# A delta-rule unit's schedule moved by two slots, and some of its VectorE work given to ScalarE

## The reference, cut to what matters

```python
L = jnp.where(strict, jnp.einsum('bhncd,bhnjd->bhncj', k_beta, k) * decay, 0.0)
a = L + jnp.eye(C, dtype=jnp.float32)
sol = lax.linalg.triangular_solve(a, rhs, left_side=True, lower=True)
u, w = sol[..., :DV], sol[..., DV:]
...
v_new = u_n - jnp.einsum('bhcd,bhde->bhce', w_n, state)
o = jnp.einsum('bhcd,bhde->bhce', q_n, state) + jnp.einsum('bhcj,bhje->bhce', attn_n, v_new)
state = state * jnp.exp(gl)[..., None, None] + jnp.einsum('bhcd,bhce->bhde', k_n, v_new)
```

## Time and profile before

| | |
|---|---|
| time of the kernel, median of 3 runs | 2789.07 us (2785.65 to 2792.15) |
| time of the profiled execution | 2786.32 us |
| its span | 2784.5 us |
| TensorE busy | 2702.4 us (97%) |
| TensorE weight load busy | 2256.1 us (81%) |
| VectorE busy | 1725.8 us (62%) |
| ScalarE busy | 561.3 us (20%) |
| GpSimd busy | 885.8 us (32%) |
| mean granted TensorE clock | 0.992 of full speed |

### The profile page before, as it was taken

The page is one execution under the profiler, slowest core; times in us unless marked ns, Lnnn a source line. Parts: engine busy times, 40 slices in busy tenths (PEclk is TensorE's granted clock), DMA queues, the critical chain, the costliest instruction groups (busy, mean ns, idle before and its releaser), DMA issues.

```text
span 2784.5 us, 38178 instructions
## 1 busy us (share of the span) xinstructions
PE 2702.4 (97%) x14098; PEld 2256.1 (81%) x14098; DVE 1725.8 (62%) x3816; ACT 561.3 (20%) x1207; POOL 885.8 (32%) x471
## 2 busy tenths in 40 slices
PE   7899999999999999999998999999999999999998
PEld 5788888888888888788777888888888888887886
DVE  5788788878854333433567797878877434443333
ACT  5222222222211111200141222222222111121001
POOL 3333233323312212434442232323333122133443
PEclk9999999999999999999999999999999999999999
DMA  4322222222211112333422322222222111133344
GB/s 164 90 64 69 67 80 64 67 66 81 70 48 39 36 40 63 125 95 114 155 82 77 81 58 74 70 77 69 62 73 75 42 46 33 40 100 96 98 132 144
DMA packets 288476, 217.71 MB, mean 78 GB/s; under 512 B 31426, under 2 KB 245780, under 8 KB 288036
## 3 DMA queue, kind: packets, MB, share of 16 engines
q1 hardware_dynamic: 255330, 154.39, 20.3%
q10 hardware_dynamic: 32962, 60.89, 6.4%
HBM read 176.37 MB, written 38.86 MB: 77 GB/s over the span
## 4 chain that ended last, share of the span: by engine, by line
PE 61%; DVE 18%; DMA 8%; issue 5%; POOL 4%; SPq 3%; ACT 1%; DVEq 0%; ACTq 0%; POOLq 0%
PE dense_ps L688 16%; PE dense_ps L692 16%; PE dense_ps L690 16%; DMA arena<-l_scratch 6%; SPq L578 2%; PE work L671 2%; DVE arena L1535 2%; DVE arena L1775 2%; DVE arena L1778 1%; DMA l_scratch<-arena 1%; DVE arena L1549 1%; POOL w_lo L2007 1%; PE work L874 1%; PE work L854 1%; POOL arena L2091 1%
## 5 line engine op out<-in xcount | busy, mean ns | idle before, releaser
L688 PE MATMUL dense_ps<-act_hi,w_hi 128*128 128x512 f32 x2816 | 1174.2, 417 | 15.9 <-POOL act_lo L2124 9.2
L692 PE MATMUL dense_ps<-act_hi,w_lo 128*128 128x512 f32 x2816 | 1106.3, 393 | 0.0
L690 PE MATMUL dense_ps<-act_lo,w_hi 128*128 128x512 f32 x2816 | 1105.0, 392 | 0.0
L2007 POOL TENSOR_TENSOR w_lo<-w_raw,w_hi 128x1024 fp32r<-128x1024 f32 x192 | 495.2, 2579 | 1328.2 <-DVE w_hi L1412 1328.2
L692 PEld LDWEIGHTS dense_ps<-act_hi,w_lo 128*128 128x128 f32 x2816 | 531.6, 189 | 117.7
L688 PEld LDWEIGHTS dense_ps<-act_hi,w_hi 128*128 128x128 f32 x2816 | 534.2, 190 | 111.6 <-POOL act_lo L2124 11.8
L690 PEld LDWEIGHTS dense_ps<-act_lo,w_hi 128*128 128x128 f32 x2816 | 534.6, 190 | 89.6 <-issue 0.2
L1535 DVE SCALAR_TENSOR_TENSOR arena<-arena,cols 128x512 f32<-128x512 f32 x288 | 273.9, 951 | 4.9
L1412 DVE CAST w_hi<-w_raw 128x1024 fp32r<-128x1024 f32 x192 | 132.9, 692 | 208.8 <-PE dense_ps L692 194.7
L671 PE MATMUL work<-mk,arena 128*128 128x128 f32 x896 | 130.3, 277 | 11.5 <-issue 7.5
L1775 DVE TENSOR_TENSOR arena<-arena 128x60 f32<-128x60 f32 (+14 forms) x480 | 99.8, 208 | 53.9 <-DMA arena<-l_scratch 41.7
(11 more groups left out here) (194 smaller groups left out, 3208.2 us busy)
## 6 DMA issues: line engine op xcount, KB each, us to landing
w_raw<-in_w_in SPq DMA_DIRECT2D x142, 512.0 KB, 3.7
arena<-l_scratch SPq DMA_DIRECT2D x32, 512.0 KB
gate_scratch<-arena ACTq DMA_DIRECT2D x64, 256.0 KB, 2.5
arena<-gate_scratch ACTq DMA_DIRECT2D x64, 256.0 KB, 2.9
w_raw<-in_w_out SPq DMA_DIRECT2D x18, 512.0 KB, 4.2
arena<-row_scratch SPq DMA_DIRECT2D x32, 256.0 KB, 5.3
o_scratch<-arena ACTq DMA_DIRECT2D x32, 256.0 KB, 2.0
arena<-o_scratch ACTq DMA_DIRECT2D x32, 256.0 KB, 3.3
```

What stands on the lines that cost most here:

```text
L688: eng.matmul(dense_ps[:, to, :], w_hi[:, slot, k, :], hi[:, k, seg], start=(k == 0), stop=False)
L690: eng.matmul(dense_ps[:, to, :], w_hi[:, slot, k, :], lo[:, k, seg], start=False, stop=False)
L692: mm = eng.matmul(dense_ps[:, to, :], w_lo[:, slot, k, :], hi[:, k, seg], start=False, stop=(k == KT - 1))
L2007: eng.tensor_tensor(w_lo[:, slot, :, :], w_from[second][:, :, :], w_hi[:, slot, :, :].bitcast(F32), ALU.subtract)\
```

## The change

1. **Slots.** In `even`, `odd` and `even_last` the solve goes from slots 3 to 7 to slots 5 to 9, `spread` from 8 to 10, the level steps from 9 to 17 to 11 to 19; in `first` the solve goes from 17 to 21 to 19 to 23 and the rest with it. `mask` and `dec` of the following unit go from 12 and 14 to 10 and 12 in `even` and `odd`; in `first` from 15 and 17 to 18 and 20, and `gram`, `keys`, `nl` of the second unit from 21, 23, 24 to 25, 26, 27. The slots without convolution steps are those of the solve, as before.
2. **ScalarE.** The copies of `level_v` 1 and 2 and of `level_x` 1 and 2, and within the units the rounding of the weight blocks (`split_hi`), are done by ScalarE.
3. **SP.** In the first unit the stores of the L blocks stand ahead of the load of weight block 3 and of the second row load; `lb` is loaded behind that weight block, and the row last.
4. `spread` has one more wait (for `xT` of the unit before, now written by ScalarE), and the first rounding of the first retention head waits for ScalarE's last one.

```diff
@@ unit_schedule, first
-        at(15, "mask", 1)
         at(16, "kq")
-        at(17, "dec", 1)
-        at(21, "gram", 1)
-        at(23, "keys", 1)
-        at(24, "nl", 1)
-        solve, spread_at, vt = 17, 22, 34
+        at(18, "mask", 1)
+        at(20, "dec", 1)
+        solve, spread_at, vt = 19, 24, 34
@@ the other kinds
-        solve, spread_at, vt = 3, 8, 19
+        solve, spread_at, vt = 5, 10, 19
+    else:
+        solve, spread_at = 0, 0
...
+    if first:
+        begin(25, 1)
...
     if kind in ("even", "odd"):
-        at(12, "mask", 1)
-        at(14, "dec", 1)
+        at(10, "mask", 1)
+        at(12, "dec", 1)
         begin(16, 1)
...
-            spread(0 if 3 <= n < 8 else 1 if n < 18 and n not in (12, 15) else 2)
+            spread(0 if solve <= n < spread_at else 1 if n < 18 and n not in (12, 15) else 2)
@@ sync
                 row_load(0, 0)
+                l_store(0, 0)
+                load_w(n + BLK_FIRST + 3, w_src(l, w_in, GR0))
+                l_load(0)
                 row_load(0, 1)
-                load_w(n + BLK_FIRST + 3, w_src(l, w_in, GR0))
-                l_blocks(0, 0)
@@ scalar
+                def split_hi(g, slot):
+                    eng.wait_ge(w_in_ok.sem, w_in_ok.after(g, 16))
+                    eng.wait_ge(dense_ok[1].sem, dense_ok[1].after(g, -1))
+                    eng.wait_ge(w_hi_ok.sem, w_hi_ok.after(g, 0))
+                    eng.activation(w_hi[:, slot, :, :], w_raw[:, :, :], ACT.Copy).then_inc(w_hi_ok.sem, 1)
...
+                        elif what == "split":
+                            idx = g0 + step[1] + 1
+                            split_hi(g + idx, idx % 2)
+                        elif what == "level_v" and step[1]:
+                            i = step[1]
+                            eng.wait_ge(v_ps.sem, v_ps.after(tn, i + 1))
+                            eng.wait_ge(xp_ps.sem, xp_ps.after(tn, i))
+                            w = 3 * P // 4 if i == 1 else LVW
+                            eng.activation(vv[0:w], wk[4][0:w, 0:CPH * LVW].rearrange("p (c t) -> p c t", c=CPH), ACT.Copy)\
+                               .then_inc(vv_ok.sem, 1)
+                        elif what == "level_x" and step[1]:
+                            ...
+                            if i == 1:
+                                eng.activation(xT[nb][0:32, :, 32:64], new[0:32, :, 0:32], ACT.Copy)
+                                eng.activation(xT[nb][64:96, :, 96:128], new[32:64, :, 32:64], ACT.Copy).then_inc(xt_ok.sem, 1)
+                            else:
+                                eng.activation(xT[nb][0:LVW, :, LVW:P], new[0:LVW], ACT.Copy).then_inc(xt_ok.sem, 1)
@@ vector
-                        elif what == "split":
-                            idx = g0 + step[1] + 1
-                            split_w(g + idx, idx % 2)
...
                         elif what == "spread":
                             eng.wait_ge(sv_s.sem, sv_s.after(tn, 2 * BASE - 2))
+                            eng.wait_ge(xt_ok.sem, xt_ok.after(tn, 0))
...
                 def ret_head(h, last):
                     m = (n + h * 6)
+                    if h == 0:
+                        eng.wait_ge(w_hi_ok.sem, w_hi_ok.after(m + BLK_RET + 5, 0))
                     split_w(m + BLK_RET + 5, (BLK_RET + 5) % 2)
```

More of the change, by code:

```diff
@@ L569, in row_load, with l_store @@
                        .then_inc(row_in.sem, 16)
-                def l_blocks(u, half):
+                def l_store(u, half):
                     t = (l * (2 * DH) + u)
@@ L578, in l_blocks, with l_load @@
                         eng.dma_start(l_dram[a].rearrange("c i k -> i c k"), nl[half][seg, :, seg]).then_inc(l_st.sem, 16)
+                def l_load(u):
+                    t = (l * (2 * DH) + u)
                     eng.wait_ge(l_st.sem, l_st.after(t, 16 * NB))
@@ L582, in l_blocks @@
                                   .to_broadcast([NB, BASE, CPH * BASE * BASE])).then_inc(l_in.sem, 16)
+                def l_blocks(u, half):
+                    l_store(u, half)
+                    l_load(u)
                 row_load(0, 0)
+                l_store(0, 0)
+                load_w(n + BLK_FIRST + 3, w_src(l, w_in, GR0))
+                l_load(0)
                 row_load(0, 1)
-                load_w(n + BLK_FIRST + 3, w_src(l, w_in, GR0))
-                l_blocks(0, 0)
                 load_w(n + BLK_HEADS, w_src(l, w_in, DK0 + P))
@@ L1227, in delta_unit @@
                                 ret_v(l * RH, gg, int(of[2]), half)
+                        elif what == "split":
[9 more added lines that the diff above has]
+                        elif what == "level_x" and step[1]:
+                            i = step[1]
+                            new = wk[5][:, 0:CPH * LVW].rearrange("p (c t) -> p c t", c=CPH)
+                            eng.wait_ge(xp_ps.sem, xp_ps.after(tn, i + 1))
+                            if i == 1:
[3 more added lines that the diff above has]
+                                eng.activation(xT[nb][0:LVW, :, LVW:P], new[0:LVW], ACT.Copy).then_inc(xt_ok.sem, 1)
                         elif what == "tanh":
@@ L1741, in delta_unit @@
                             i = step[1]
-                            eng.wait_ge(v_ps.sem, v_ps.after(tn, i + 1))
                             if i == 0:
+                                eng.wait_ge(v_ps.sem, v_ps.after(tn, i + 1))
                                 level = mk[:, C_LV + i * LVW:C_LV + (i + 1) * LVW].unsqueeze(1).to_broadcast([P, CPH, LVW])
@@ L1746, in delta_unit @@
                                                   ALU.mult).then_inc(vv_ok.sem, 1)
-                            else:
-                                eng.wait_ge(xp_ps.sem, xp_ps.after(tn, i))
-                                w = P - LEVELS[i]
-                                eng.tensor_copy(vv[0:w], wk[4][0:w, 0:CPH * LVW].rearrange("p (c t) -> p c t", c=CPH))\
-                                   .then_inc(vv_ok.sem, 1)
                         elif what == "level_x":
                             i = step[1]
-                            eng.wait_ge(xp_ps.sem, xp_ps.after(tn, i + 1))
-                            new = wk[5][:, 0:CPH * LVW].rearrange("p (c t) -> p c t", c=CPH)
                             if i == 0:
+                                eng.wait_ge(xp_ps.sem, xp_ps.after(tn, i + 1))
                                 part = lower(xT[nb].rearrange("p c t -> p (c t)"), i)
@@ L1759, in delta_unit @@
                                                   ALU.add).then_inc(xt_ok.sem, 1)
-                            elif i == 1:
-                                eng.tensor_copy(xT[nb][0:32, :, 32:64], new[0:32, :, 0:32])
-                                eng.tensor_copy(xT[nb][64:96, :, 96:128], new[32:64, :, 32:64]).then_inc(xt_ok.sem, 1)
-                            else:
-                                eng.tensor_copy(xT[nb][0:LVW, :, LVW:P], new[0:LVW]).then_inc(xt_ok.sem, 1)
                         elif what == "solve":
```

## The result

The changed kernel takes 2869.7 us in the median (2868.8 to 2870.2) against 2789.2 us before (2785.7 to 2792.2): ratio 1.0288, 95% interval 1.0268 to 1.0308, so it is 2.9% slower. One run of the changed kernel was disturbed (4498.8 us, clock 0.56) and is left out. The profiled execution took 2868.8 us with a span of 2867.0 us, 82.5 us more than the one before.

The account below looks back on a forecast made before the run. TensorE, busy for 2702 of 2784 us, was taken to bound the kernel. Old waits -24, solve held by GpSimd +117, clock +24 and first units -5 gave +112 on the median 2789.1: 2901 us, range 2765 to 2955.

Parts of the forecast that it names:

- the likeliest case: Whole kernel: the forecast that GpSimd holds the solve, 2901 us, own range 2850 to 2950, chance 0.55.
- The solve meets GpSimd: From slot 8: `w_lo`, starting at 17.0 us, and both masks hold solve steps on VectorE; +117 us (93 to 138).
- What it costs, 3.9 us a unit: TensorE's waits for `uu` and `spread`: 3.9 us a unit (3.1 to 4.6), 30 units, +117 us.
- -24 us for the old waits: Solve two slots later: the wait on `lb` and TensorE's before L904 and L915 go, -24 us (-30 to 0).
- +24 us for the clock: TensorE's clock falls behind the new waits: 0.8 us each, 30 times, +24 us.
- Rounding at slot 0: On ScalarE, ahead of the copy of the new values: costs TensorE 0 to 0.2 us a unit, taken as 0.
- rival C: ScalarE as new obstacle: copy behind rounding, tanh behind `dec`, up to 1 us a unit; 2790 us, chance 0.05.
- First units, -5 us: First unit of each layer: shorter waits and clock loss, -10.5, less 5.5 for masks holding the solve; -5 (-15 to +5).
- Masks two slots earlier, 0: Masks and `dec` two slots earlier: moves nothing by itself, 0, bounds -0.3 and +0.5 us a unit.
- What counts is what the rounding released.: Second rounding on ScalarE at slot 8 no longer follows solve and `spread`, so `w_lo` and masks meet the solve; +117 us.
- Rival A: No meeting: solve over before GpSimd matters, or short instructions slip in between; only gains stay, 2763 us, chance 0.22.

Follow-up runs that it names:

- rounding back on VectorE: Changed kernel with the unit roundings back on VectorE in its order; slots, level copies and SyncE's order as changed: 2936.1 us.
- slots of before: Changed kernel with the earlier kernel's slots (solve from slot 3, `spread` at 8); roundings and level copies still on ScalarE, SyncE's order as changed: 2756.6 us.
- second rounding behind `spread`: Changed kernel with the second rounding kept on ScalarE but moved from slot 8 to 11, waiting for `spread`; mask and `dec` at 12 and 14: 2870.7 us.
- one more GpSimd instruction: Changed kernel with one more GpSimd instruction of 128x512 behind the masks (the second mask written twice): 2924.5 us.
- first unit unheld: Against slots of before: in first units, masks in slot 22 waiting for `spread`, later `dec`, `gram`, `keys`, `nl`; weight block HEADS+1 loaded ahead of the stores: 2749.5 us.

## Why the prediction was right, and where its numbers were off

The class and the mechanism were right: forecast 2901 us, measured 2869.7, inside the range and inside the likeliest case's own (2850 to 2950). That the number came as near as 31 us is in part luck: units and clock were put 44 us too high (141 against 97.3 us, the holds of the first even units included), and 15.7 us came from a wait that the sum does not have.

- **The solve meets GpSimd.** Right, to the instruction: `w_lo` was put 17.0 us behind the unit's start, and it came at 17.5 (475.44 - 457.91). The three holds of 2.2, 0.9 and 1.0 us above the normal length are there in the unit shown, and three such in every even and odd unit. Taking the masks away, adding one instruction, and moving the solve by one slot changed the number of holds as counted.
- **What it costs, 3.9 us a unit.** The mis-sized term. The 28 ordinary units lose 90.0 us, 3.2 each, restarts of TensorE and clock included, where I had 4.7 with the clock. The step that failed is the count "at +2.1 nine small instructions are left" and that `uu` "stands behind the third of them": seven were left, and `uu` stood behind the first, so it was out at +2.7 us from the start of `w_lo` and TensorE waited 1.0 us for it, not 4.5. The other two holds cost 1.2 us at `level_v` 0, since GpSimd was through 4.9 us from the start of `w_lo`, not 5.4. I had 3.9 us for a VectorE that is two instructions ahead, which it was; there I had left `uu` behind the second hold by mistake, when two ahead puts it behind the first.
- **-24 us for the old waits.** Right: the loss of all 30 units before was 27.8 us, and its causes are gone (L914 1.0 us, no wait on `lb`).
- **+24 us for the clock.** Wrong, near 0 in ordinary units: waits of 1.0 and 1.2 us left it at 1.00. It follows at least in part from the size above: with waits of 1.0 and 2.2 us it fell to 0.50 in 10 of 18 units, and behind one of 3.1 us or more in all 28 even and odd units of the run with the rounding back on VectorE. The mean clock of the profile is 0.990 (0.992 before).
- **Rounding at slot 0, "0 to 0.2 us a unit".** Right in the ordinary units, wrong in the two first even ones, where the block had not landed. I had ruled that SP's other queue entries keep their order; they do, but one of them stood behind stores that wait for the moved `nl`. That is +15.7 us, rival C in one place. I had moved a step without following the queue it feeds.
- **First units, -5 us.** -3.3 us. The masks fell on the convolution ahead of the solve (three L1571 took 6.15 us together), and the `w_lo` of the next block (92.90 us) on the solve, 2.27 us on k=11; TensorE's wait is 5.34 us against 5.62.
- **Masks two slots earlier, 0.** Right, by the run that puts them back.
- **"What counts is what the rounding released."** Half right. Released early, `w_lo` is the better place for it as long as the solve is over by then: that alone made the kernel before 18.8 us faster (2766.9 against the 2785.7 us measured beside it). It hurts only together with the solve's two slots, and the slots hurt more without it (2936 us). Rival A's own condition, a `w_lo` later against the solve, is met with the solve two slots earlier, and A's number (2763) is near what came (2757), though not by A's sum: A has 5 to 10 us from the first units, which gave 0.7 us there.

The Trainium skill, page "SBUF — State Buffer" (section "SBUF: two separate sides"), says that whichever of the two starts first holds the pair for its whole instruction and the other fully blocks. Every hold shown here agrees, the one of four elements a partition (L1844, 1.24 us) too, which a sharing of bandwidth could not stretch so. One thing does not, as far as the profile's lengths of GpSimd's instructions go: under the power of 128x4 elements (L2116, 1.02 us) the convolution's first instruction (L1568) began 14 times in the changed kernel, and 14 times it took its usual 0.48 us and ended before it.

## What to carry to other kernels

Where VectorE and GpSimd work side by side, lay GpSimd's SBUF instructions as intervals over VectorE's order and ask what stands under each: an instruction on the critical chain is held for as long as GpSimd's lasts. A convolution with slack is held for nothing where nothing urgent stands behind it in VectorE's order (slots of before), and costs 2.7 us where `level_x` 0 does (second rounding behind `spread`). Before a step is moved, list what it was protected from by standing where it stood, and every queue entry that waits for it (here one weight load behind two stores, 16 us). And take the parts of a bundled change apart: without its slots this one is 1.2% faster than the kernel before, 0.75% by the rounding on ScalarE alone, and that hid in a change that was 2.9% slower.

## What was not expected of the hardware

- In the units shown the holds follow each other: `w_lo` and the masks hold the second instruction of k=11, the first and the second of k=12. The held instruction is done as GpSimd's ends, and the next one with two SBUF inputs is held by the next of GpSimd's. Two SBUF inputs are not the whole criterion: the convolution's first instruction, which reads one tensor in SBUF and a column, took 1.12 instead of 0.49 us under `w_lo` (L1569, slots of before), while a reduction of 128x512 in SBUF kept its 0.69 us under it (L1840 in the run with the late rounding, 14 of 14). Behind the second mask, with GpSimd's own wait of about 0.1 us ahead of the added instruction, one solve instruction slipped through (k=13 first, 0.17 us).
- An instruction that reads PSUM and one SBUF operand (`uu`, 0.34 us) ran at its normal length under a mask.
- The same waits of TensorE did not always do the same to the clock. It stayed at full behind 1.0 and 1.2 us in all 27 units that have these, and fell to 0.50 behind a single 3.1 to 3.5 us in all 28 even and odd units of the run with the rounding back on VectorE. In between it went both ways: behind 1.0 and 2.2 us it fell in 10 units and stayed in 8 (one more GpSimd instruction), and behind a single 2.53 us it stayed in layer 0 and fell in layer 1 (first unit unheld).
